# Gated delta rule: one run of block products for both scan directions, with the backward halves exchanged in ScalarE's copy

## The reference, cut to what matters

```python
def gated_delta_chunked(q, k, v, beta, g):       # b, h, n = 8 chunks, c = 64
    gcum = jnp.cumsum(g, axis=-1)
    decay = jnp.exp(jnp.where(incl, gcum[..., :, None] - gcum[..., None, :], -jnp.inf))
    k_beta = k * beta[..., None]
    a_kk = jnp.where(strict, jnp.einsum("bhnid,bhnjd->bhnij", k_beta, k) * decay, 0.0)
    t_inv = lax.linalg.triangular_solve(eye + a_kk, eye, lower=True, unit_diagonal=True)
    u = jnp.einsum("bhnij,bhnjd->bhnid", t_inv, v * beta[..., None])
    w = jnp.einsum("bhnij,bhnjd->bhnid", t_inv, k_beta * jnp.exp(gcum)[..., None])
    ...                                          # then a scan over the chunks with a 64x64 state

def bidir_gated_deltanet(q, k, v, beta, g):      # forward, and backward on the flipped sequence
    return fwd + flip(gated_delta_chunked(flip(q), flip(k), flip(v), ...))
```

## Time and profile before

| | us |
|---|---|
| median of 3 runs | 3355.74 |
| range of the runs | 3354.07 to 3357.53 |
| the profiled execution: its own time | 3356.01 |
| its span from first to last instruction | 3354.2 |
| TensorE busy in it | 3197.8 (95%) |
| VectorE busy | 1879.4 (56%) |
| ScalarE busy | 1411.8 (42%) |
| GpSimd busy | 429.9 (13%) |

### The profile page before, as it was taken

How to read it: one execution, slowest core, us unless ns; L and a number is a source line. 1 busy time by engine, 2 the same in 40 slices (tenths; PEclk the granted TensorE clock), 3 DMA queues, 4 the chain that set the end, 5 groups by cost and what they waited for, 6 DMA issues and landing times.

```text
span 3354.2 us, 60527 instructions
## 1 busy us (share of the span) xinstructions
PE 3197.8 (95%) x26204; PEld 2527.9 (75%) x26204; DVE 1879.4 (56%) x2890; ACT 1411.8 (42%) x2478; POOL 429.9 (13%) x444
## 2 busy tenths in 40 slices
PE   8898889999999898999999999999999999999999
PEld 6577777888876677778888876767788767676887
DVE  6566657666466665556746564553444555535443
ACT  5544233433245444333423354554433455544432
POOL 0051430000000240520000000121201001204010
PEclk9899999999999899999999999999999999999999
DMA  4001113333331001023333332212132222121223
GB/s 150 33 22 40 40 34 108 103 98 97 94 119 58 20 22 52 28 69 105 100 95 94 96 128 66 73 45 70 60 91 70 90 82 87 52 66 60 76 79 98
DMA packets 75210, 249.09 MB, mean 74 GB/s; under 512 B 9281, under 2 KB 10945, under 8 KB 73921
## 3 DMA queue, kind: packets, MB, share of 16 engines
q1 hardware_dynamic: 74944, 245.22, 23.1%
HBM read 237.88 MB, written 6.29 MB: 73 GB/s over the span
## 4 chain that ended last, share of the span: by engine, by line
PE 83%; DVE 7%; ACT 4%; POOL 3%; issue 2%; DMA 0%; SPq 0%; POOLq 0%; DVEq 0%; ACTq 0%
PE psum L521 80%; PE psum L703 3%; POOL s_xb L2673 2%; DVE s_xb L1962 1%; DVE s_tmp L1965 1%; ACT s_tmp L1258 1%; POOL s_tmp L2673 1%; ACT s_E L1258 1%; DVE s_nm L2046 1%; ACT s_whi L1258 1%; DVE s_wlo L1962 1%; DVE s_ffy L1965 0%; PE psum L608 0%; DVE s_tmp L1962 0%; ACT s_PT L1258 0%
## 5 line engine op out<-in xcount | busy, mean ns | idle before, releaser
L521 PE MATMUL psum<-s_h,s_whi 128*128 128x512 f32 (+1 forms) x4576 | 1464.4, 401 | 26.7 <-DVE s_tmp L1965 18.0
L521 PEld LDWEIGHTS psum<-s_h,s_whi 128*128 128x128 f32 (+1 forms) x4576 | 853.0, 190 | 237.9 <-issue 48.3
L521 PE MATMUL psum<-s_h,s_wlo 128*128 128x512 f32 (+1 forms) x2288 | 899.5, 393 | 0.0
L1962 DVE TENSOR_TENSOR s_wlo<-s_stage,s_whi 128x1024 fp32r<-128x1024 f32 (+2 forms) x468 | 527.9, 1130 | 356.9 <-ACT s_whi L1258 355.6
L1258 ACT ACTIVATE s_whi<-s_stage 128x1024 fp32r<-128x1024 f32 (+2 forms) x468 | 449.8, 966 | 251.8 <-DMA s_stage<-wdn 66.9
L521 PEld LDWEIGHTS psum<-s_h,s_wlo 128*128 128x128 f32 (+1 forms) x2288 | 432.8, 189 | 96.0
L521 PE MATMUL psum<-s_ffa,s_whi 128*128 128x512 f32 x704 | 217.5, 390 | 4.6 <-DVE s_ffa L1962 4.6
L2705 POOL TENSOR_SCALAR s_E<-s_E,s_inv,s_g 128x128 f32<-128x128 f32 (+3 forms) x128 | 77.1, 613 | 1069.6 <-DVE s_inv L2066 1048.4
L2673 POOL TENSOR_TENSOR s_xb<-s_xb,s_cstm 64x512 f32<-64x512 f32 x64 | 91.8, 1435 | 919.3 <-DVE s_xb L1962 914.9
L2046 DVE TENSOR_REDUCE s_nm<-psum 128x1 f32<-128x512 f32 (+3 forms) x288 | 137.6, 520 | 112.1 <-PE psum L521 111.4
L1965 DVE SCALAR_TENSOR_TENSOR s_ffy<-psum,s_pcol,s_ffy 128x511 f32<-128x511 f32 x176 | 131.7, 748 | 110.8 <-ACT s_ffy L1258 107.7
(11 more groups left out here) (298 smaller groups left out, 4368.5 us busy)
## 6 DMA issues: line engine op xcount, KB each, us to landing
s_stage<-w SPq DMA_DIRECT2D x192, 512.0 KB, 3.6
s_stage<-wup SPq DMA_DIRECT2D x88, 512.0 KB, 3.5
s_stage<-wo SPq DMA_DIRECT2D x32, 512.0 KB, 3.5
s_stage<-wdn SPq DMA_DIRECT2D x32, 512.0 KB, 3.5
s_stage<-wdn SPq DMA_DIRECT2D x16, 384.0 KB, 3.1
spill<-s_x SPq DMA_DIRECT2D x2, 2048.0 KB, 8.4
s_stage<-woa SPq DMA_DIRECT2D x16, 256.0 KB, 2.6
s_x<-spill SPq DMA_DIRECT2D x2, 2048.0 KB, 8.0
```

The lines of the kernel that those rows point to most:

```text
L521: return self.e.matmul(out, left, right, start=first, stop=last, skip_group_check=True)
L1962: return self.e.tensor_tensor(out, a, b, op)
```

## The change

In a round, P of both directions is now issued in one run, when direction 1 has its turn: `blocks` takes both PSUM banks, waits for C and X of both directions, and then goes through the products with the directions alternating, n, then a, then r. Direction 0 stays crossed, direction 1 is now uncrossed. The four products of one `n` so go through all four quadrants. Since direction 1's P now lies in the halves that it was read from, ScalarE's copy exchanges them: two copies of 64 partitions take the place of one of 128. Products, masks, updates, banks and filler are otherwise as they were.

```diff
@@ Tensor.unit
         for b in range(1, 6):
-            C = self.tmp((key, "C", b))
-            ps = self.take((key, "P", b))
-            self.w.wait_ge(*self.at("pool_unit", key, "C", b))
-            self.w.wait_ge(*self.at("vec_unit", key, "X", b - 1))
-            self.eight(ps, C, X, True).then_inc(*self.up("pe_unit", key, "P", b))
-            self.give((key, "P", b), ("act_unit", key, "P", b))
+            if r == 1:
+                self.blocks((l, g, jp), b)
             yield
@@ Tensor
+    def blocks(self, both, b):
+
+        ps = [self.take(((*both, r), "P", b)) for r in range(2)]
+        for r in range(2):
+            self.w.wait_ge(*self.at("pool_unit", (*both, r), "C", b))
+            self.w.wait_ge(*self.at("vec_unit", (*both, r), "X", b - 1))
+        for n in range(8):
+            for a in range(2):
+                for r in range(2):
+                    last = self.one(ps[r], self.tmp(((*both, r), "C", b)), self.m.slot[r][0], a, n, r == 0)
+                    if (n, a) == (7, 1):
+                        last.then_inc(*self.up("pe_unit", (*both, r), "P", b))
+        for r in range(2):
+            self.give(((*both, r), "P", b), ("act_unit", (*both, r), "P", b))
@@ Scalar.unit
             self.w.wait_ge(*self.at("pe_unit", key, "P", b))
-            self.f(Pm, self.bank((key, "P", b)), ACT.Copy).then_inc(*self.up("act_unit", key, "P", b))
+            ps = self.bank((key, "P", b))
+            if r == 0:
+                self.f(Pm, ps, ACT.Copy).then_inc(*self.up("act_unit", key, "P", b))
+            else:
+                self.f(Pm[half(0)], ps[half(1)], ACT.Copy).then_inc(*self.up("act_unit", key, "P", b, 0))
+                self.f(Pm[half(1)], ps[half(0)], ACT.Copy).then_inc(*self.up("act_unit", key, "P", b))
```

## The result

The changed kernel takes 3362.11 us (median of 20 runs, 3356.42 to 3371.72) against 3355.69 us for the kernel before, measured beside it (20 runs). The ratio is 1.0019, with a 95% interval of 1.0011 to 1.0027: slower by about 6.4 us, where 3.7 us faster had been forecast, and 1.1 us above the upper end of the range. Twelve runs in a later job gave 3362.24 us and a ratio of 1.0009 (0.9999 to 1.0019). So the loss is 3 to 6 us, and the forecast gain is absent in both.

A forecast was written before the change was run, and what follows sets the result against it. TensorE, busy 95% of the span with 83% of the chain, was taken to bound the kernel. Classes of rounds summed to 5.9 us gained, the clock cost 2: 3352.1 us profiled, median about 3352, range 3344 to 3361 us.

The forecast's parts named there:

- filler both sides: Ten rounds with filler before and behind P: filler and XY hide the extra copy, P's gain stays, -10.3 us.
- no filler after P: Six rounds where XY follows P directly: the gain becomes a wait for the copy, 0.05 us lost each, +0.3 us.
- no filler either side: Four rounds with P between two XYs: direction 0's copy starts later, 1.0 us lost each, +4.0 us.
- second rounds without filler: Two second rounds behind a wait in group 1, without filler on either side: 0.5 us lost each, +1.0 us.
- TensorE waits already: Twelve rounds where TensorE already waits for VectorE: the new run ends when the old did, -0.9 us together.
- ScalarE holds XY: Six rounds in group 0's second pair, where a table load in ScalarE's queue delays the copies: 0 us.
- the clock: Second rounds with longer TensorE waits: two more stretches at half clock, 2.2 us less what hides, +2 us, between 0 and 14.
- the ten rounds: The rounds with filler on both sides of P, forecast to gain 10.3 us.
- slower by the clock: Rival: eight longer waits, at two second rounds and six runs without filler, each bring half clock, 13.6 us: 3364 us, chance 0.10.
- So all 1.03 us stay: Ten rounds with filler on both sides: three updates end 0.3 us ahead of the next P, keeping the whole 1.03 us.
- Copies 0.49 us apart: ScalarE's copies in a row: each takes 0.60 us, starting 0.49 us apart, so the third adds 20 us to ScalarE's work.
- XY's 16.4 ns: Price of a packed P record, from XY's pace: 64 take 1.05 us instead of 2.08, 41 us less TensorE work in all.

The follow-up runs named there:

- e7: Changed kernel with overwritten 128x256 products filling TensorE's waits ahead of P in first and second rounds of three of four pairs: 3352.75 us, ratio 0.9987.
- e9: Changed kernel with e7's 54 added products made 32 x 1, hardly any work, at the same places: 3358.49 us, ratio 1.0000.
- e3: Kernel before with P packed and the copy split only in the ten rounds with filler on both sides: 3352.75 us, ratio 0.9988.
- e2: Changed kernel with direction 1's P copied in one piece, without exchanging its halves: 3357.41 us, ratio 0.9998.
- e15: e2 with e7's overwritten products added: 3353.82 us, ratio 0.9987.
- e16: Changed kernel with 24 products of 32 x 1 at one place in each layer, ahead of P's joint wait: 3358.98 us, ratio 1.0008.
- the cold forms: Changed kernel in its two measurements, e16 and e9, all without e7's overwritten products: ratios 1.0019, 1.0009, 1.0008 and 1.0000.
- e12: Kernel before with 32 products of 32 x 1 once in each layer, ahead of the first unit's wait for VectorE: 3364.89 us, ratio 1.0020.

## Why the prediction was wrong, step by step

The 40 rounds by the prediction's classes, from the one profiled execution of each kernel. Measured is, for every round, the time from the last product of the XY before it (in a first round from the last product ahead of it) to the last of its own XY, less the same in the kernel before. The last column is e7, in which the clock's part is largely gone.

| class | forecast | changed kernel | e7, warm |
|---|---|---|---|
| filler both sides, 10 | -10.3 | -6.1 | -7.1 |
| no filler after P, 6 | +0.3 | +1.3 | -0.8 |
| no filler either side, 4 | +4.0 | +6.8 | +3.0 |
| second rounds without filler, 2 | +1.0 | +4.0 | +0.6 |
| TensorE waits already, 12 | -0.9 | +3.5 | -1.0 |
| ScalarE holds XY, 6 | 0 | -3.4 | +0.3 |
| sum | -5.9 | +6.1 | -5.0 |
| the clock | +2 | (in the rows above) | (little left) |

As wholes these executions differ from the kernel before's by +2.4 and -2.2 us. Most of the rest lies where nothing was changed: ahead of the first unit, at 163 us, TensorE is already 2.2 us behind the kernel before in the changed kernel and 4.2 us in e7, and behind 1480 us it makes up 5.1 and 3.7 us. One pair of executions can't be read more finely than that, and the medians decide.

With the clock kept up the sum, -5.0, is nearly the -5.9 forecast without it, and e7's measured 4.4 us agrees. In the main the latencies of the new order were right, but that the sums agree so well is partly luck: the ten rounds give 3.2 us less than forecast, and stretches at half clock and pauses that the kernel before had in other rounds make up for it. **The step that failed is the clock's term.** The prediction put it at +2 us for two more stretches; there were nine more.

- **The clock, +2 us.** The prediction looked for long waits in second rounds, because the earlier trace rows shows one there, and charged two more stretches. But the change joins the two waits of the *first* round, 2.19 us for P and 1.12 us for XY, which had work between them, into one of 3.2 to 3.3 us with all of the unit's work behind it. Seven of the 19 stretches follow there (251.93, 386.46, 1231.56, 1368.02), four behind second rounds whose wait grew from 2.4 to 3.6 us (at 455.85 and 1436.66); at the second rounds of the earlier trace rows's kind the kernel before had four. Nine more stretches than before, not two. What e7 wins back is 7 and 11 us against the changed kernel's two measurements, each give or take 4, and 2 us is outside both; against the control e9 it is 4 us, give or take 4. It is the rival "slower by the clock", which had a chance of 0.10 and named 3364 us and eight stretches, with price and count nearly right and the places in part wrong: it had looked for them at two second rounds, where they came, and around missing filler.
- **The ten rounds, -10.3 us.** The mechanism was right. P's gain is 0.92 us each, not 1.03, because P takes 1.16 us and XY's pace leaves out the last record's length: 9.2 us. The other 2 to 3 us go to pauses and to filler and XY that take longer in single rounds, half clock among it. In e3 more is given back at a place where VectorE sets the moment anyway. "So all 1.03 us stay" holds to the next unit, not to the end.
- **Copies 0.49 us apart.** They are 0.62 us apart, so direction 1's XY is 0.30 us late in the undisturbed rounds without filler behind P (XY takes 2.39 us at 1385.21, and 2.09 us at the same place, 1379.30, in e2 without the third copy). That is 1.8 us instead of 0.3 for six rounds. In e7's column a pause of 1.3 us that the kernel before had in one of these rounds is gone, which hides it.
- **No filler on either side, +4.0 us.** Undisturbed rounds lose 1.25 us (1.2 of wait ahead of P and 0.16 in XY, less 0.10), not 1.0; the 6.8 us of the changed kernel hold 2.2 us more in XY, most of it half clock (at 480.6 and 1269.0 us).
- **TensorE already waits, -0.9 us, and ScalarE holds XY, 0.** Both hold with the clock kept up (-1.0 and +0.3).
- **P packed.** At half clock it takes 1.98 us, hardly less than the 2.08 us of an unpacked P at full clock. A packed round that falls to half clock so keeps 0.1 us of its 0.92.

The Trainium skill's floor of about 25 ns between starts of products ("TensorE: Matmul & The Clock Gate", section "Wait — 56ns, not 53.3ns?") was set aside for XY's 16.4 ns, and the new P bears that out: 64 records in 1.16 us to the end of the last.

Shown by runs: that packing pays in the ten rounds and costs in the thirty; that the order alone costs 10 us; that work in the waits turns the changed kernel from slower to faster. That it does so by the clock is shown by the clocks of all runs (0.981 to 0.988) and by e9, e15 and e16, which leave neither the added instructions nor the pauses as the cause of all of it. Open is the size: how much of the 7 to 11 us between the changed kernel and e7 is the clock's, since the control e9 came out at 1.0000 and the four ratios of the cold forms overlap. The clocks don't give it either. At 0.983 three runs of the changed kernel took 3356 to 3358 us and 17 of the kernel before 3362.5 us (median), as if all but the clock gained 5 us; but at e7's 0.988 nine runs of the kernel before took 3350.9 us, no more than e7. Open as well is why the third copy seems to cost only in the cold kernel.

## What to carry to other kernels

Before two waits of one engine are joined ahead of its work, add up what stood between them: a wait of 3.3 us where 2.2 and 1.1 us stood cost next to nothing in latency (0.0 to 0.2 us in these rounds of e7), but the work behind it may run at half clock. The clock's term must be looked for at every wait that the change lengthens, the first of a chain above all, and read as busy time and granted clock of the stretch behind it. Where such a wait can't be avoided, products whose result is overwritten, in a bank that the engine has already taken, bought the clock back here. Pack only the rounds where other work covers the copies, and let the rest alone.

## What the runs showed of the hardware

- 64 records of 64x64 fp32 products through four quadrants take 1.16 us at full clock and 1.98 us at half, not twice as long.
- ScalarE's copies of 64 partitions take as long as those of 128 (591 and 597 ns), but three copies in a row, two of them exchanging halves, start 0.62 us apart, 0.54 us without the exchange, two whole ones 0.49 us apart. By form, the half copies of the changed kernel:

```profile
L1269 ACT ACTIVATE s_xb<-psum 64x512 f32<-64x512 f32 x80 | 47.3, 591 | 1.9
```

- A product of 32 x 1 elements is not free: 64 records took 3.54 us in one bank with one stationary block, 55 ns each (e12), where 64x64 records through four quadrants start 16 ns apart.
- TensorE pauses of 0.3 to 2 us that no semaphore explains follow packets of the instruction queue by 1.9 to 3.1 us: all seven beside the units of the kernel before do, and 86 other packets there are followed by none. That they are waits for instructions is inferred from this coincidence; no run here forced it.
- The mean granted clock differs from run to run of one kernel (0.981 to 0.989 in 161 runs of the kernel before), and the time with it, by 2.1 us for every 0.001. An execution that is traced should be placed among the others by it.
